# Starts of the SBUF tensors moved to multiples of 2048 bytes, and a scratch of 2048 bytes

## The reference

```
proj = rmsnorm(h) @ w_in            # first block, per layer: 1024 x 5656
h = h + concat(y_hg, y_nsa) @ w_out
h = h + sigmoid(rmsnorm(h) @ w_pg) * (p @ w_pp)
...
h = x @ w_in; g, u = split(h)       # second block: feed-forward, twice per layer
x = layer_norm(a * x + 0.5 * (silu(g) * u) @ w_out)      # width 2816
... # differential attention (layer 0) or a pooling mixer (layer 1),
... # then attention over 256 memory tokens, each with its projections
```

## Time and profile before

| | us |
|---|---|
| median of 3 runs | 3623.47 |
| lowest, highest | 3599.29, 3647.61 |
| profiled execution | 3616.13 |
| its span, first to last instruction | 3614.3 |
| TensorE busy (share of the span) | 3243.3 (90%) |
| POOL, VectorE, ScalarE busy | 1369.7, 1251.1, 1105.5 |
| mean granted TensorE clock, of full speed | 0.946 |

### The profile page before, as it was taken

How to read it: one execution, slowest core, us unless ns; L and a number is a source line. 1 busy time by engine, 2 the same in 40 slices (tenths; PEclk the granted TensorE clock), 3 DMA queues, 4 the chain that set the end, 5 groups by cost and what they waited for, 6 DMA issues and landing times.

```text
span 3614.3 us, 59291 instructions
## 1 busy us (share of the span) xinstructions
PE 3243.3 (90%) x24262; PEld 2907.5 (80%) x24262; DVE 1251.1 (35%) x2127; ACT 1105.5 (31%) x1835; POOL 1369.7 (38%) x651
## 2 busy tenths in 40 slices
PE   5988898997799899989788898999899987889997
PEld 5985476997358899979447878999799975789997
DVE  2026654106564311050576053110411058251103
ACT  2232433222253322132253333221322233332222
POOL 4433014443103344444403624444444444244442
PEclk9988899998799999999898999999999998999999
DMA  4320012331001232313101412222232331213231
GB/s 160 93 70 18 1 30 76 96 102 36 6 1 59 77 99 93 99 57 105 35 1 58 134 46 74 92 93 96 64 99 93 100 101 57 70 60 101 95 99 53
DMA packets 72068, 261.86 MB, mean 72 GB/s; under 512 B 7920, under 2 KB 8560, under 8 KB 70800
## 3 DMA queue, kind: packets, MB, share of 16 engines
q1 hardware_dynamic: 70048, 250.32, 21.8%
q10 hardware_dynamic: 1904, 9.94, 0.8%
HBM read 258.13 MB, written 2.10 MB: 72 GB/s over the span
## 4 chain that ended last, share of the span: by engine, by line
PE 77%; DVE 15%; ACT 3%; issue 3%; POOL 1%; DMA 0%; SPq 0%; DVEq 0%; ACTq 0%; POOLq 0%
PE bank L405 22%; PE bank L409 21%; PE bank L407 21%; PE bank L644 2%; PE bank L670 2%; DVE tb L1352 1%; PE bank L635 1%; DVE sg L1341 1%; PE bank L582 1%; PE bank L818 1%; DVE s L1302 1%; ACT wh L883 1%; PE bank L576 1%; PE bank L508 1%; DVE proj L1464 1%
## 5 line engine op out<-in xcount | busy, mean ns | idle before, releaser
L319 POOL TENSOR_TENSOR wl<-raw,wh 128x1024 fp32r<-128x1024 f32 x464 | 1153.9, 2503 | 1876.3 <-ACT wh L883 1876.2
L405 PE MATMUL bank<-xh,wh 128*128 128x256 f32 x5120 | 1017.4, 280 | 106.8 <-POOL xl L333 77.6
L407 PE MATMUL bank<-xl,wh 128*128 128x256 f32 x5120 | 1010.5, 279 | 0.0
L409 PE MATMUL bank<-xh,wl 128*128 128x256 f32 x5120 | 1009.7, 279 | 0.0
L405 PEld LDWEIGHTS bank<-xh,wh 128*128 128x128 f32 x5120 | 783.5, 190 | 124.1 <-issue 94.3
L883 ACT CAST wh<-raw 128x1024 fp32r<-128x1024 f32 x464 | 468.3, 1047 | 1043.4 <-PE bank L409 1010.6
L407 PEld LDWEIGHTS bank<-xl,wh 128*128 128x128 f32 x5120 | 783.7, 190 | 0.0
L409 PEld LDWEIGHTS bank<-xh,wl 128*128 128x128 f32 x5120 | 781.9, 190 | 0.0
L405 PE MATMUL bank<-hh,wh 128*128 (+1 forms) x1408 | 279.3, 280 | 5.8 <-ACT sg L1132 5.8
L409 PE MATMUL bank<-hh,wl 128*128 (+1 forms) x1408 | 279.3, 280 | 0.0
L407 PE MATMUL bank<-hl,wh 128*128 (+1 forms) x1408 | 279.0, 280 | 0.0
(11 more groups left out here) (301 smaller groups left out, 3613.3 us busy)
## 6 DMA issues: line engine op xcount, KB each, us to landing
raw<-in_slabs SPq DMA_DIRECT2D x464, 512.0 KB, 3.5
h<-in_x_t SPq DMA_DIRECT2D x1, 2048.0 KB, 8.4
w1v<-in_w ACTq DMA_DIRECT2D x2, 1024.0 KB, 4.8
side<-in_pp_w ACTq DMA_DIRECT2D x2, 1024.0 KB, 4.8
xm<-in_mem_t ACTq DMA_DIRECT2D x2, 1024.0 KB, 4.8
out<-h SPq DMA_DIRECT2D x8, 256.0 KB, 2.0
side<-in_w SPq DMA_DIRECT2D x1, 1024.0 KB, 14.2
vt<-in_p_t ACTq DMA_DIRECT2D x2, 512.0 KB, 3.6
```

The lines of the kernel that those rows point to most:

```text
L319: nc.gpsimd.tensor_tensor(wl[:, n % RING, :], raw[:, n % RING, :], wh[:, n % RING, :], A.subtract).then_inc(w_low, 1)
L405: nc.tensor.matmul(dst[:, c], high_l, high_r[:, c], start=first and n == 0, stop=False)
L407: nc.tensor.matmul(dst[:, c], high_l, low_r[:, c], start=False, stop=False)
L409: out = nc.tensor.matmul(dst[:, c], low_l, high_r[:, c], start=False, stop=last and n == len(parts) - 1)
```

## The change

Two fillers that nothing reads or writes are put among the tensors, 1920 bytes ahead of h and 64 bytes after lam, and the scratch for DMA descriptors is made 2048 bytes. h then starts at byte 4096 (2048 of scratch, 128 of constants, 1920 of filler; before: 16512). In bytes past a multiple of 2048 the starts become: h, raw, wh, wl and cst 0; sg, tb, sq, s1, s2 and w1v 224; xh, xl, hh, hl, proj, vt, dq, xq, xk and blocks_k 0; blocks_v 1920; side 1408. All tensors lie some 12,400 bytes lower than before. No instruction is added, removed or moved on any engine.

```diff
@@ -179,6 +179,7 @@
+        keep("fore_room", [P, 2048 - 128], mybir.dt.uint8)
         h = keep("h", [P, KC, T])
         raw = keep("raw", [P, RING, D])
         wh = keep("wh", [P, RING, D], f32r)
@@ -200,6 +201,7 @@
         ksm = keep("ksm", [P, 3, 64])
         lbt = keep("lbt", [P, 4, 4])
         lam = keep("lam", [P, 4])
+        keep("mid_room", [P, 64], mybir.dt.uint8)
@@ -1962,7 +1964,7 @@
-    nc = bacc.Bacc("TRN2", target_bir_lowering=False, num_devices=1)
+    nc = bacc.Bacc("TRN2", target_bir_lowering=False, num_devices=1, dynamic_dma_scratch_size=2048)
```

## The result

The changed kernel takes 3713.98 us in the median (3713.29 to 3715.96, 4 runs) against 3614.98 us for the kernel before (3599.29 to 3647.61, 4 runs): the ratio is 1.0263, with a 95% interval of 1.0188 to 1.0337. It is slower, and it has become steady: its four runs lie 2.7 us apart, those of before 48 us.

The account below looks back on a forecast made before the run. The prediction took TensorE to bound the kernel, by the time from one matmul's start to the next. All four parts summed to 0 on 3616.1 us; a middle with the runs' median 3623.5 gave 3620 us, range 3570 to 3675.

Parts of the forecast that it names:

- (1): TensorE's operand reads in 21312 matmuls: moving the starts costs 0, bounds 31 us less to 61 us more.
- rival B: Slower: TensorE's reads, or its read and ScalarE's write, meet at congruent starts; 4.44 ns a product, 91 us, 3707 us; chance 0.06.
- the argument from alternation: In TensorE's products, if crossing a multiple of 2048 cost time, intervals would alternate; they do not, so 0.
- the witnesses: TensorE's L508 takes 421 ns at different starts; L809 has congruent operands 64 past a multiple and no toll.
- all slow: Upper bound for TensorE's products: every stage gets the slow rate, 117.78 ns, 61 us more.
- Its sign: Rival B would show as fewer than 830 matmuls in 100 us windows inside TensorE's long stages.
- Its alternative: Within rival B: TensorE's read meets ScalarE's write of the next tile, also a 4.44 ns step a product.
- Rival A: Faster: off a boundary each TensorE product pays a toll over 108 ns; 140 us would go, 3476 us; chance 0.10.
- (2): VectorE, ScalarE and POOL instructions at moved starts: taken as 0, VectorE's share bounded at 11 us either way.
- (4): Smaller scratch for DMA descriptors: nothing late for want of it, nothing sooner, 0.
- (3): DMA transfers of slabs: worth 0 in the loop, 0.3 us either way at the start; taken as 0.
- Rival C: The two rates are dealt anew to TensorE's stages, by change or chance: 3585 to 3677 us; chance 0.24.

Follow-up runs that it names:

- e2: Kernel before with 2048 bytes of scratch and fillers putting ring and h at 0, activations at 64 past a multiple of 2048: 3663.62 us, ratio 1.0107.
- e3: Kernel before with 2048 bytes of scratch and fillers putting ring and activations both 64 past a multiple of 2048: 3714.99 us, ratio 1.0255.
- the first probe: Without the model: trains of 48 products of 256 columns at various starts of weights and moving operand; fp32r took 113.3, 117.8 or 120.0 ns a product.
- e1: Kernel before with the smaller scratch of 2048 bytes alone, no filler: 3628.42 us against 3622.18, ratio 1.0009.
- e4: Kernel before with 2048 bytes of scratch and fillers putting ring at 0, activations at 192 (distance 192): 3618.89 us, ratio 1.0013.
- e6: Kernel before with 2048 bytes of scratch and fillers putting ring at 0, activations at 256 past a multiple of 2048: 3713.9 us in one run.
- e7: The changed kernel with each product in one matmul of 512 columns instead of two of 256: 3589.14 us, ratio 0.9897 to the kernel before.
- e5: Kernel before with 2048 bytes of scratch and a filler putting activations at 0, ring at 128 (distance 128): 3694.13 us, ratio 1.0212.
- e8: Kernel before with each product in one matmul of 512 columns instead of two of 256: 3656.41 us, ratio 1.0083.
- own: Probe train without the model, starts alternating between 0 and 64, each moving operand at distance 0 from its own weights: 116.7 ns with 256 columns.
- next: Probe train without the model, starts alternating, each moving operand 64 from its own weights, 0 from the next matmul's: 116.7 ns with 256 columns.

## Why the prediction was wrong

The forecast was 3620 us in 3570 to 3675, and the time was 3714: rival B, to which I gave 0.06, happened.

*The step that failed is (1), TensorE's reads, taken as 0 with +61 us as the upper bound.* Its size was 106 us. The runs showed in its place that a product's interval hangs on the distance of its two operands, and that distance 0 costs 120.0 ns where 192 costs 113.3 or 117.8. Three things went wrong in the step. First, the argument from alternation was sound for what it tested, a toll for crossing a multiple of 2048, and e2 and e3 bear it out: it isn't the boundary that costs. But I took its failure for the failure of every effect of the start. What counts is the distance of the two operands, and it was one and the same, 192, in all products of `pair` and the feed-forward. The 1344 products in which wh or wl is the moving operand had 64, at which the same two rates occur, so no pattern in the trace could show it. Second, the witnesses were of the wrong type. L508 and L809 are fp32, and the first probe has fp32 at 216 ns and bf16 at 109.1 to 109.2 at all three distances tried (0, 64 and 192). L809, congruent and untolled, was my main point against B; the prediction's last sentence named this gap, and I did not let it weigh. Third, the bound: "all slow" took the slower of two rates seen for the slowest there is. A third stood 2.22 ns above it.

*Rival B* had the condition, congruent starts of weights and moving operand, and nearly the price: 4.44 ns for each of 20595 products, 91 us and 3707 us, against 106 us in the intervals. The step was 6.67 ns on the fast kind and 2.22 on the slow kind instead of 4.44 on each. So part of the nearness is luck. Its sign, fewer than 830 matmuls in a window, did not come either: 836, which a step of 4.44 ns on the fast kind (851) would not give. That the two reads meet in the memory is not shown; what is shown is that the interval goes with the distance of their starts. Its alternative, that ScalarE's writes are met, is not needed: the probes have the 120.0 ns without them.

*Rival A* priced the excess over 108 ns a product, half of an fp32 record's 216. By the first probe such a record is itself half of a matmul, so that the 108 had no ground. The excess does hang on the starts, but 113.3 is the least that any distance gave with 256 moving and 128 weight columns, and the boundary removed nothing. The Trainium skill (TensorE: Matmul & The Clock Gate, "Wait — 56ns, not 53.3ns?") gives 2.5 ns over the columns, by estimate 109.2 ns for 256. bf16 in the first probe meets it with 109.1 to 109.2, and fp32r, which has 6.7 to 13.3 ns over the columns, does not.

*(2)* held in size: the busy times of VectorE, ScalarE and POOL changed by under 4 us. The 1276 ns that I set against 1262 as a possible effect of h's start were chance: e1, with the starts of before, has a shortest of 1263 in that group. *(4)* held by e1. *(3)* held in size: a slab lands in 3.5 us after as before, and the first slabs' part of the chain went from 9.07 us to 8.70:

```profile
2.93 8.70 DMA raw<-in_slabs
```

Over all versions, one execution each, that part is 8.65 to 8.88 us with the ring on a multiple of 256 (the change, e2, e4, e6, e7), 8.98 to 9.21 with it 128 past one (before, e1, e5, e8), and 8.87 with it 64 past one (e3). By the rule of the Trainium skill, DMA: Bandwidth & Descriptors, "How a descriptor splits into AXI transactions", every start off a multiple of 256 should cost, by estimate about 0.5 us. The runs with 128 agree in direction, with 0.3 us between the means, and e3 does not; either way it is worth nothing here.

*Rival C* probably tells why the runs of the kernel before spread. The runs of before spread over 24 to 48 us each time they were taken, those of e1 and e4, at the same distance, over 32. Every version in which one rate holds for four products in five or more (the change, e2, e3, e5, e7, e8) keeps within 9, though over only four to six runs. Only one execution of each was profiled, so that the mix in the others is not known. Of those profiled, e1 had 1866 more slow intervals than before, worth 8.3 us, and took 9.1 us more; e4 had 295 more, worth 1.3, and took 5.5 more. So the mix gives most of the one difference and little of the other.

What stays open: what happens between the two reads, and with which load, since "own" and "next" cost the same; why 96 costs what 0 does; and what decides at distances 64 and 192 between 113.3 and 117.8 ns when a train or a stage begins.

## What to carry to other kernels

For fp32r products on TensorE, look at the distance of the starts of weights and moving operand and not at either start alone, and price it with a probe of that very number type and width: a trace in which nearly all instructions share one distance says nothing of it, however regular it is. Round numbers are no safe choice, since they make everything congruent. And when a layout and an instruction's width interact, as here, try them together: the alignment that lost 2.6% with halves won 1.0% with whole tiles.

## What the runs showed of the hardware that I had not expected

- An fp32r matmul of 256 columns with a load of 128 weight columns comes every 113.3, 117.8 or 120.0 ns, or in mixtures between, by the distance of its operands modulo 256 bytes; fp32 (216 ns a record, two records a matmul) and bf16 (109.1 to 109.2 ns) were the same at distances 0, 64 and 192.
- At distances 64 and 192 two rates are stable for hundreds of microseconds with nothing different in the code. The kernels at 192 differed by 0.7 to 1.3% from run to run, those at all other distances or widths by 0.1 to 0.25%, in fewer runs.
- With 512 columns the order of the distances changes: 0 is the best (226.8 ns) and 192, with 256 columns as good as any, is among the worst (233.3; the worst is 160 with 234.3).
- Fewer weight columns don't always make it faster: at distance 192 an fp32r matmul of 256 columns took 119.0 ns with 64 weight columns, and 113.3 or 117.8 with 128.
